# A fused transformer kernel on one core: three weight buffers start 32 bytes off a 64-byte line

## The reference, cut to what matters

```
h = h + (silu(hn @ w_gate) * (hn @ w_up)) @ w_down        # first block, layer "gu"

def swiglu(h, w_gu, w_down):                              # second block, layers "gu1" and "gu2"
    a, b = jnp.split(h @ w_gu, 2, axis=-1)
    return (jax.nn.silu(a) * b) @ w_down
```

## Time and profile before

| | us |
|---|---|
| median of three runs | 2005.5 |
| lowest, highest | 2004.41, 2006.53 |
| span of the profiled execution | 2004.3 |
| TensorE matmuls busy | 1982.4 |
| TensorE weight loads busy | 1717.1 |
| VectorE busy | 1236.5 |
| GpSimd busy | 905.8 |
| ScalarE busy | 898.6 |

### The profile page before, as it was taken

How to read it: one execution, slowest core, us unless ns; L and a number is a source line. 1 busy time by engine, 2 the same in 40 slices (tenths; PEclk the granted TensorE clock), 3 DMA queues, 4 the chain that set the end, 5 groups by cost and what they waited for, 6 DMA issues and landing times.

```text
span 2004.3 us, 32457 instructions
## 1 busy us (share of the span) xinstructions
PE 1982.4 (99%) x11622; PEld 1717.1 (86%) x11622; DVE 1236.5 (62%) x1937; ACT 898.6 (45%) x1605; POOL 905.8 (45%) x458
## 2 busy tenths in 40 slices
PE   9999999999999999999999999999999999999998
PEld 7788788878999988899998888887777888999887
DVE  4675885346788787877768774463552247777111
ACT  4334444344566522556652252225663245666322
POOL 3344323326577655544445434443224445444443
PEclk9999999999999999999999999999999999999999
DMA  6243212212333286333338635322222223333321
GB/s 209 90 152 106 74 64 83 86 33 94 106 105 105 95 314 247 101 115 105 105 95 326 237 120 149 116 95 85 68 70 85 89 89 95 105 105 105 103 98 63
DMA packets 67246, 234.71 MB, mean 117 GB/s; under 512 B 7632, under 2 KB 9040, under 8 KB 66640
## 3 DMA queue, kind: packets, MB, share of 16 engines
q1 hardware_dynamic: 66432, 232.29, 35.3%
q10 hardware_dynamic: 720, 1.15, 0.2%
HBM read 225.54 MB, written 2.10 MB: 114 GB/s over the span
## 4 chain that ended last, share of the span: by engine, by line
PE 94%; DVE 3%; ACT 1%; issue 1%; DMA 0%; POOL 0%; SPq 0%; POOLq 0%; DVEq 0%; ACTq 0%
PE bank L2254 12%; PE bank L2255 12%; PE bank L2260 12%; PE bank L2433 9%; PE bank L2434 9%; PE bank L2437 9%; PE bank L2378 5%; PE bank L2379 5%; PE bank L2384 5%; PE bank L2228 1%; PE bank L2230 1%; PE bank L2229 1%; PE bank L2552 1%; PE bank L2560 1%; PE bank L2553 1%; PE bank L2870 1%
## 5 line engine op out<-in xcount | busy, mean ns | idle before, releaser
L538 POOL TENSOR_TENSOR wlo<-raw,whi 128x1024 fp32r<-128x1024 f32 x233 | 579.9, 2490 | 807.7 <-ACT whi L657 807.4
L657 ACT ACTIVATE whi<-raw 128x1024 fp32r<-128x1024 f32 x233 | 245.8, 1057 | 475.0 <-PE bank L2384 217.7
L2254 PE MATMUL bank<-xh,whi 128*128 128x512 f32 x764 | 302.0, 395 | 1.2 <-DVE xl L1355 0.9
L2255 PE MATMUL bank<-xl,whi 128*128 128x512 f32 x764 | 297.7, 390 | 0.0
L2378 PE MATMUL bank<-hh,whi 128*128 (+1 forms) x480 | 186.9, 389 | 1.0 <-ACT whi L657 1.0
L2379 PE MATMUL bank<-hl,whi 128*128 (+1 forms) x480 | 186.8, 389 | 0.0
L2260 PE MATMUL bank<-xh,wlo 128*128 128x512 f32 x736 | 181.6, 389 | 0.0
L2254 PEld LDWEIGHTS bank<-xh,whi 128*128 128x128 f32 x764 | 143.5, 188 | 34.9 <-issue 4.7
L2255 PEld LDWEIGHTS bank<-xl,whi 128*128 128x128 f32 x764 | 143.5, 188 | 29.5 <-issue 0.7
L2260 PEld LDWEIGHTS bank<-xh,wlo 128*128 128x128 f32 x736 | 138.1, 188 | 28.9
L2434 PE MATMUL bank<-xl,whi 128*128 128x256 f32 x648 | 162.5, 283 | 0.0
(11 more groups left out here) (396 smaller groups left out, 4510.0 us busy)
## 6 DMA issues: line engine op xcount, KB each, us to landing
raw<-units SPq DMA_DIRECT2D x341, 512.0 KB, 3.7
ada_w<-ada_rows SPq DMA_DIRECT2D x72, 512.0 KB, 5.6
h<-x_t SPq DMA_DIRECT2D x8, 256.0 KB, 5.3
out_t<-h SPq DMA_DIRECT2D x8, 256.0 KB, 2.1
raw<-units SPq DMA_DIRECT2D x4, 256.0 KB, 4.5
mem_in<-mem_t SPq DMA_DIRECT2D x1, 1024.0 KB, 11.2
turned_q<-proj SPq DMA_DIRECT2D x4, 256.0 KB, 5.1
dec<-decays SPq DMA_DIRECT2D x4, 256.0 KB, 4.7
```

The lines of the kernel that those rows point to most:

```text
L538: pool.tensor_tensor(wlo[:, j % 2 * UNIT:(j % 2 + 1) * UNIT], raw[:, j * UNIT:(j + 1) * UNIT], whi[:, j % 2 * UNIT:(j % 2 + 1) * UNIT].bit ...
L657: act.activation(whi[:, v % 2 * UNIT:(v % 2 + 1) * UNIT], raw[:, slot * UNIT:(slot + 1) * UNIT], ACT.Copy).then_inc(hi_ready, 1)
L2254: mm(bank[:, 0:n], wh, chunk(rhs[0], t, n), start=t == 0, stop=False)
L2255: mm(bank[:, 0:n], wh, chunk(rhs[1], t, n), start=False, stop=False)
```

## The change

Three buffers get a start address 32 bytes further on: `half_line` is 1/32 KB. To make room for the last 32 bytes, 16 columns (64 bytes) are put behind `ssum` and 16 behind `side`. What is taken after `ssum` moves by 64 bytes, and what is taken after `side` by 128. The order of the instructions on every engine is the same, word for word.

```
         xn = sb("xn", 2 * T)
-        ssum, rstd = sb("ssum", T), sb("rstd", T)
+        ssum = sb("ssum", T)
+        sb("ssum_trail", 16)
+        rstd = sb("rstd", T)
...
-        side = sb("side", 12 * 256)
+        side = sb("side", 12 * 256 + 16)
         arena = sb("arena", arena_kb * 256)

         arena_at = nc.sbuf_base - arena_kb * 1024
-        side_at = arena_at - 12 * 1024
+        side_at = arena_at - 12 * 1024 - 64
+        half_line = 1 / 32
...
-        w_t1 = at("w_t1", 8, 8 * P, f32r, base=side_at)
-        w_t2 = at("w_t2", 0, 8 * P, f32r, base=xn_at)
-        w_t3_high = at("w_t3_high", 4, 4 * P, f32r, base=xn_at)
+        w_t1 = at("w_t1", 8 + half_line, 8 * P, f32r, base=side_at)
+        w_t2 = at("w_t2", half_line, 8 * P, f32r, base=xn_at)
+        w_t3_high = at("w_t3_high", 4 + half_line, 4 * P, f32r, base=xn_at)
```

## The result

| | before | after |
|---|---|---|
| median of five runs, us | 2005.5 | 2014.18 |
| lowest, highest | 2004.26, 2006.53 | 2012.97, 2016.15 |
| span of the profiled execution | 2004.3 | 2012.4 |

The changed kernel is slower: the ratio is 1.0046, with a 95% interval of 1.0035 to 1.0057. The forecast was 2001.0 us with a range of 1999.3 to 2005.2. Both its sign and its range were wrong.

What follows compares the result with a forecast made beforehand. TensorE's matmul pace was taken to bound the kernel. Displaced weights were to save 97.0 ns a pair, less the present 13.3: 83.7 ns over 54 pairs, 4.5 us off the median 2005.5, giving 2001.0 us, range 1999.3 to 2005.2.

Steps and rivals of the forecast that it cites:

- What bounds the kernel: Whole kernel: TensorE works 1982.4 of 2004.3 us, so only matmul pace or a TensorE wait moves the end.
- The reading of the four `w_t_low` matmuls: T3's low part in fast pairs: weights 32 bytes off a 64-byte line give 280 ns matmuls against 283.
- The present saving: Fast pairs before the change: four displaced weights already save 13.3 ns a pair, 3.33 ns each.
- The price of each: Displaced matmuls in fast pairs: 2.5 ns saved each, 6 for a run's last; 83.7 ns more a pair, 4.5 us.
- The other addresses: Buffers moved by 64 or 128 bytes, whole lines: cost 0, bounded at 6.5 us for matmuls reading S1, S2, S4.
- The Trainium skill: Its separate read ports for weights and streamed operand would make addresses irrelevant, sum 0; kept as a rival against the trace.
- The engines that write the buffers: VectorE writes off a line take 692 ns against 683; hidden behind 0.49 us slack, so cost 0.
- R4: VectorE's reads off a line in fast pairs slow down: at least 2011.8 us if doubled; chance 0.07, shared with moved operands.
- R1: Each displaced load in the fast pairs saves the whole 3.33 ns: 1999.7 us, period 9.960 us; chance 0.24.
- R2: Long runs in fast pairs settle back to a slow rhythm after some eight matmuls: 2003.5 to 2004.8 us; chance 0.20.
- R3: Separate ports hold and `w_t_low` is fast for another reason; no change, 2005.5 us; chance 0.07.
- R4 or a cost from the moved moving operands: The slower outcome: VectorE's reads off a line, or streamed operands at moved addresses, cost time; chance 0.07.

Runs made afterwards that it cites:

- e7: The kernel before with the arena alone moved by 32 bytes, which also puts `w_t3_low` on a 64-byte line: 2021.23 us, ratio 1.0078.
- e10: The kernel before with every buffer moved by 32 bytes, none against another: 2004.25 us, ratio 0.9997.
- e3: The kernel before with every buffer moved by 128 bytes, none against another: 2005.09 us, ratio 0.9998.
- e4: e1 without the weights' 32 bytes; the streamed sums (and `w_t1` with them) stay 64 bytes on, the arena 256: 2002.98 us, ratio 0.999.
- e5: The changed kernel with streamed sums moved by 256 bytes and the arena by 512, so only the weights' 32 bytes are left: 2002.44 us, ratio 0.9988.
- e9: e1 with the fast pairs' `whi` and `wlo` slots also shifted by 32 bytes, one down, one up: 1999.14 us, ratio 0.9969.
- e2: The kernel before with only the arena and what is behind it moved, by 128 bytes: 2017.95 us, ratio 1.0066.
- e1: The changed kernel with 128 bytes more between side and arena, so the arena stands 256 bytes on from before: 2001.73 us, ratio 0.9984.

## Why the prediction was wrong, point by point

**What bounds the kernel.** Right: TensorE's pace sets the end, and no other engine does. From there, though, I read only the groups of the fast pairs, whose weights move.

**The reading of the four `w_t_low` matmuls.** Wrong in its cause. I compared them with the other groups by one number, the start modulo 64 of the weights. The same list of addresses held another difference: `w_t3_low` is the only buffer of weights whose start differs from that of its streamed operand by something other than a multiple of 256. e7 and e10 refute the first, and e3, e4, e5, e9 and e10 support the second.

**The present saving** (13.3 ns a pair) stands. **The price of each** came out near by luck: the pair was to take 9.983 us and took 9.960 to 9.969, but 10.014 where only the weights' 32 bytes were left (e5). By themselves they bring 0.053 of the 0.084 us forecast. Either move alone brings half to two thirds of the pair's gain (e5, e4), since a product is out of step as soon as one of its two operands has moved, though in e4 some products in step gained too. The T4 product and the plain products beside it gained as well, which I had put at 0.

**"The other addresses ... I take 0."** This is the step that failed, and with it the sign. I called 64 and 128 bytes "whole lines" and so without effect. My bound, 6.5 us, counted only the 36 matmuls a pair that read S1, S2 and S4, 256 columns each, and for those the effect was a gain. The arena, moved by 128 bytes, is streamed by some 2500 matmuls of 512 columns, in the down projections and the projections from `yh`, `yl` and `oh`. On average they lost 5 to 6 ns each in the changed kernel; moved alone, the arena costs 12.8 us (e2). "Nothing in the rows points to it" was true only because no row of a 512-column matmul was among them. Multiplied out, 3.33 ns on each of these 2500 would have been a bound of 8 us, more than the forecast gain.

**The Trainium skill**, in "TensorE: Matmul & The Clock Gate", section "Step-by-step: what each phase is for", gives the streaming operand and the weights independent read ports, so that loading the next weights takes no read bandwidth from the running matmul. What I drew from it in the prediction, that addresses could not matter, does not hold in the runs: with the same instructions and data the pace changes when one operand moves and not when both do (e2 against e3, 1.0066 and 0.9998). Whether the read ports are where the two meet, no run shows.

**The engines that write the buffers, and R4.** The cost of 0 was nearly right. VectorE's reads off a line last 684 ns at the median, against 683:

```profile
L1615 DVE TENSOR_TENSOR w_t<-bank,w_t x108: 675/684/693, 514.8 to 1862.0; 128x512 fp32r<-128x512 f32 x108
```

The 692 ns into `w_t_low` were no price of writing off a line either. The kernel before takes about as long into `wlo`, which is on a line, and e10 has `w_t_low` on a line and still takes 692. First the kernel before, then e10:

```profile
L1612 DVE TENSOR_TENSOR wlo<-bank,whi x54: 672/690/692, 522.8 to 1861.7; 128x512 fp32r<-128x512 f32 x54
```

```profile
L1613 DVE TENSOR_TENSOR w_t_low<-bank,w_t_high x54: 673/692/693, 516.2 to 1860.3; 128x512 fp32r<-128x512 f32 x54
```

R4 named the right sign with a mechanism that is not there. The slack ahead of the left tokens' product is 0.32 us (0.49 before): the sum is done at 564.43, and the product starts at 564.75.

```profile
564.02 0.41 DVE L1626 TENSOR_TENSOR tmp<-bank,tmp 128x256 f32<-128x256 f32 x1
...
564.75 0.28 PE L2436 MATMUL bank<-s,w_t 128*128 128x256 f32 x1
```

So the slack shrinks more than "hardly" when TensorE gets faster. In about half of gu's 18 pairs it is down to 0.21 us; in 8 of them the second matmul of the product starts 137 to 158 ns after the first, where about 118 is usual, 0.2 us in all. That fits gu's 9.969 beside gu1's 9.960. I did not test it by itself.

**R1** gave the period (9.960) exactly, and that was luck, by a wrong account: the full rate on 36 matmuls, where it was more matmuls at less each. **R2** saw a real relapse to 120 ns after about 8 matmuls; e4 shows it in products in step, and none in T2 and T4, which are out of step. **R3**, no change, fell.

**Chances.** "R4 or a cost from the moved moving operands" had 0.07, on a bound that had left out most of the moved reads.

## What to carry to other kernels

An edit that takes a few bytes more for a buffer moves everything behind it, and matmul pace here depended on where the streamed operand starts against the weights, modulo 256 bytes. Pad each such edit to a multiple of 256 bytes, or list for every product both starts before and after, and count all matmuls that read a moved buffer, not those of the loop in question. Where one group is faster than its like, list all that differs before naming the cause, and test on the group with the most instructions.

## What the runs showed of the hardware

- Matmuls of 512 columns (fp32r, 128 x 128 weights loaded for each) follow each other at 227 ns with operands in step. With the arena moved by 32, 64, 128 or 192 bytes those of `hh` and `hl` average 232 to 233 ns (`hh` by `whi` up to 234.4), and those of `yh` and `yl` 233, or 229.4 at 64 bytes.
- With 256 columns it is the reverse: 120 ns in step (loads 192 ns), and 117 to 119 in whole products out of step (loads mostly 187 to 188 ns). At 128 bytes the memory's products hardly gain (119.1 against 119.3).
- Out of step the fast pace holds through whole products, on average. In step it lasts up to some 8 matmuls, behind products out of step (e4) or after a pause. In e9, where all seven products of the pair are out of step, a few groups still are slow (`s_hi` by `whi_up` 284 ns, `w_t_low` 283).
- An offset common to both operands played no part: 128 bytes (0.9998) and 32 bytes (0.9997).
- The step is 256 bytes, as far as distances were tried: `hh` lies an even multiple of it from `whi` before (65024 = 254 x 256) and an odd one in e1 (65280 = 255 x 256), both at 227 ns, and 128 bytes off is slow (e2).
- Not settled: why the two sizes go opposite ways, and why 64 bytes cost less than 192. No run separated a conflict of reads in the memory from one in the engine, nor the distance to a matmul's own weights from that to the next ones, which are loaded while it runs.
